# Between two layers of a fused diffusion block: the layer's output scaled as its bank is emptied, and the next layer's first weight halves split in other places and partly on GpSimd

## The reference, cut to what matters

```
h  = modulate(rmsnorm(x, norm_mix_pre), shift, scale)
z  = h @ w_in                                  # 24 tiles of 128 columns
m  = merge_branches(h, four mixers of z) @ w_o
x  = x + mod[2] * rmsnorm(m, norm_mix_post)
f  = conv_ffn(modulate(rmsnorm(x, norm_ffn_pre), ...)) # ends in @ w_down
x  = x + mod[5] * rmsnorm(f, norm_ffn_post)
```

## Time and profile before

| | |
|---|---|
| median of 3 runs | 1653.98 us (1651.18 to 1657.06) |
| the profiled execution's own time | 1649.58 us |
| its span, first to last instruction | 1647.8 us |
| TensorE busy | 1590.0 us, 96% |
| VectorE busy | 932.1 us, 57% |
| ScalarE busy | 789.6 us, 48% |
| GpSimd busy | 309.6 us, 19% |
| mean granted TensorE clock | 0.990 of full speed |
| chain that ended last | TensorE 70%, VectorE 3%, ScalarE 3% |

### The profile page before, as it was taken

How to read it: one execution, slowest core, us unless ns; L and a number is a source line. 1 busy time by engine, 2 the same in 40 slices (tenths; PEclk the granted TensorE clock), 3 DMA queues, 4 the chain that set the end, 5 groups by cost and what they waited for, 6 DMA issues and landing times.

```text
span 1647.8 us, 33059 instructions
## 1 busy us (share of the span) xinstructions
PE 1590.0 (96%) x14076; PEld 1323.8 (80%) x14076; DVE 932.1 (57%) x1481; ACT 789.6 (48%) x1299; POOL 309.6 (19%) x248
## 2 busy tenths in 40 slices
PE   8999999998899999999999999999989899999998
PEld 6788767777678887888888886987877789889987
DVE  5364455564465569655554225655776265677764
ACT  4322456473354266443443225525766344566653
POOL 0160234323110000212222000312352120012210
PEclk9999999999999999999999999999999899999999
DMA  9753334233852352322225343833413295555453
GB/s 332 201 164 102 101 105 160 75 103 96 268 201 89 107 193 76 103 96 84 98 69 111 105 125 125 262 128 116 147 52 130 55 317 169 187 172 180 164 189 133
DMA packets 213840, 234.41 MB, mean 142 GB/s; under 512 B 5888, under 2 KB 194688, under 8 KB 213696
## 3 DMA queue, kind: packets, MB, share of 16 engines
q1 hardware_dynamic: 194208, 191.14, 35.3%
q0 software_dynamic: 14880, 34.87, 7.9%
q10 hardware_dynamic: 4608, 6.29, 1.1%
HBM read 216.55 MB, written 15.73 MB: 141 GB/s over the span
## 4 chain that ended last, share of the span: by engine, by line
PE 70%; DVE 3%; issue 3%; ACT 3%; DMA 1%; POOL 0%; ACTq 0%; DVEq 0%; POOLq 0%
PE ps L2333 15%; PE ps L2335 15%; PE ps L2334 15%; PE ps L2795 2%; PE ps L2629 2%; PE ps L2641 2%; PE ps L2424 1%; PE ps L2681 1%; PE ps L2398 1%; PE ps L2399 1%; PE ps L2400 1%; PE ps L2603 1%; PE ps L2788 1%; PE ps L2790 1%; PE ps L2789 1%
## 5 line engine op out<-in xcount | busy, mean ns | idle before, releaser
L1062 ACT ACTIVATE whi<-ring 128x1024 fp32r<-128x1024 f32 (+1 forms) x262 | 274.4, 1052 | 488.7 <-PE ps L2335 428.2
L1607 DVE TENSOR_TENSOR wlo<-ring,whi 128x1024 fp32r<-128x1024 f32 (+1 forms) x262 | 327.4, 1254 | 176.2 <-ACT whi L1062 175.4
L2333 PE MATMUL ps<-H,whi 128*128 128x256 f32 (+1 forms) x640 | 214.7, 336 | 1.8 <-DVE wlo L1607 1.8
L2335 PE MATMUL ps<-H,wlo 128*128 128x256 f32 (+1 forms) x640 | 214.2, 335 | 0.0
L2334 PE MATMUL ps<-H,whi 128*128 128x256 f32 (+1 forms) x640 | 214.2, 335 | 0.0
L2333 PE MATMUL ps<-HR,whi 128*128 128x512 f32 (+1 forms) x568 | 202.1, 356 | 0.5 <-DVE wlo L1607 0.3
L2335 PE MATMUL ps<-HR,wlo 128*128 128x512 f32 (+1 forms) x568 | 198.3, 349 | 0.0
L2334 PE MATMUL ps<-HR,whi 128*128 128x512 f32 (+1 forms) x568 | 198.2, 349 | 0.0
L2333 PEld LDWEIGHTS ps<-H,whi 128*128 128x128 f32 x640 | 121.5, 190 | 14.0 <-issue 1.9
L2335 PEld LDWEIGHTS ps<-H,wlo 128*128 128x128 f32 x640 | 121.5, 190 | 12.3
L2334 PEld LDWEIGHTS ps<-H,whi 128*128 128x128 f32 x640 | 121.5, 190 | 12.2
(11 more groups left out here) (399 smaller groups left out, 3219.2 us busy)
## 6 DMA issues: line engine op xcount, KB each, us to landing
ring<-in_ffn_up SPq DMA_DIRECT2D x44, 1024.0 KB, 5.0
ring<-in_w_gate SPq DMA_DIRECT2D x32, 1024.0 KB, 5.7
ring<-in_ada_w SPq DMA_DIRECT2D x32, 1024.0 KB, 5.3
ring<-in_w_in SPq DMA_DIRECT2D x24, 1024.0 KB, 7.9
ring<-in_ffn_down SPq DMA_DIRECT2D x10, 1024.0 KB, 5.0
ring<-in_ffn_down SPq DMA_DIRECT2D x18, 512.0 KB, 3.6
ada<-in_ada_w SPq DMA_DIRECT2D x8, 1024.0 KB, 11.6
WB<-in_w_branch POOLq DMA_DIRECT2D x8, 1024.0 KB, 6.3
```

The source lines that it names most:

```text
L1062: act.activation(whi[HALF_SLOT[m]][:, 0:kn, :], ring_half(raw, half, kn), ACT.Copy).then_inc(hi_done, 1)
L1607: dve.tensor_tensor(wlo[HALF_SLOT[m]][:, 0:kn, :], ring_half(raw, half, kn), whi[HALF_SLOT[m]][:, 0:kn, :].bitcast(F32), ALU.subtract).the ...
L2333: pe.matmul(o[:, c0:c1], hi[:, i, :], part(0, k), start=(k == 0), stop=False)
L2335: last = pe.matmul(o[:, c0:c1], lo[:, i, :], part(0, k), start=False, stop=(k == kn - 1))
```

## The change

Five things, all between the last product of layer 0 and the first of layer 1:

1. ACT scales `F` by `amod[:, 3]` as it empties the bank, in two instructions of 256 columns per tile instead of one of 512. The residual's second step becomes one addition of 512 columns, `X = X + F`.
2. DVE's modulation biases and the gains of layer 1's first norm move from behind the residual into it, behind the addition of its fifth tile. The four small scales move ahead of layer 0's down projection.
3. ACT splits the first high part behind the square of the fifth tile, the second behind that of the sixth, and the third behind the root of the second norm.
4. The three low parts are made by GpSimd, behind its last product of layer 0 and ahead of layer 1's bias loads.
5. DVE counts the three halves as made and waits for them behind `norm_apply`.

```diff
+SPLIT_BEHIND = (4, 5)
...
@@ gpsimd, behind the loop over FT
+                if l == 0:
+                    first_z = half_no(("z", 1, Z_ORDER[0]))
+                    for m in range(first_z, first_z + SPLIT):
+                        raw, half = HALVES[m]
+                        pool.wait_ge(lo_done, m)
+                        pool.wait_ge(hi_done, m + 1)
+                        pool.tensor_tensor(wlo[HALF_SLOT[m]][:, :, :], ring_half(raw, half),
+                                           whi[HALF_SLOT[m]][:, :, :].bitcast(F32), ALU.subtract).then_inc(lo_done, 1)
@@ scalar
                 for i in range(KT if l else 0):
                     act.wait_ge(x_ready, 8 + i + 1)
                     square(YB[:, i, :], X[:, i, :])
+                    if i in SPLIT_BEHIND:
+                        split_until(half_no(("z", l, Z_ORDER[0])) + SPLIT_BEHIND.index(i) + 1)
                 if l:
+                    norm_root(l, 0)
                     split_until(half_no(("z", l, Z_ORDER[0])) + SPLIT)
-                    norm_root(l, 0)
...
                     square(SQF[:, j, c0:c1], s[:, c0:c1])
-                    act.activation(F[:, j, c0:c1], s[:, c0:c1], ACT.Copy).then_inc(frees(("down", l, j)), 1)
+                    if j == 0:
+                        act.wait_ge(gains_ready, 4 * l + 3)
+                    for x in streams(l):
+                        ins = act.activation(F[:, j, 256 * x:256 * x + 256], s[:, 256 * x:256 * x + 256], ACT.Copy,
+                                             scale=amod[:, 3, j, x:x + 1])
+                    ins.then_inc(frees(("down", l, j)), 1)
@@ vector, residual
-                        for s in streams(l):
-                            x = X[:, i - 1, 256 * s:256 * s + 256]
-                            ins = dve.scalar_tensor_tensor(x, O[:, i - 1, 256 * s:256 * s + 256],
-                                                           amod[:, k, i - 1, s:s + 1], x, ALU.mult, ALU.add)
+                        x = X[:, i - 1, c0:c1]
+                        if k == 3:
+                            ins = dve.tensor_tensor(x, x, O[:, i - 1, c0:c1], ALU.add)
+                        else:
...
                         ins.then_inc(x_ready, 1)
+                    if k == 3 and i == 5:
+                        fill(("end", l, 0))
+                        gains(l + 1, (0,))
@@ vector, start of a layer
-                if l:
-                    gains(l, (0,))
-                link(dve.tensor_scalar(omu[:, :], vc(l, "mu", 0, 14), -1.0, 1.0, ALU.mult, ALU.add))
...
-                if l:
-                    split_until(half_no(("z", l, Z_ORDER[0])) + SPLIT)
+                if l == 0:
+                    layer_scales(0)
+                else:
                     norm_apply(l, 0, X, Z, HR)
                     fill(("gap", l, 0))
+                    halves[0] += SPLIT
+                    dve.wait_ge(lo_done, halves[0])
@@ vector, ahead of the down projection
+                layer_scales(l + 1)
```

More of the change, by code:

```diff
@@ L1637, in _, with layer_scales @@
             called = [0]
+            def layer_scales(l):
+                link(dve.tensor_scalar(omu[:, :], vc(l, "mu", 0, 14), -1.0, 1.0, ALU.mult, ALU.add))
+                link(dve.tensor_scalar(oka[:, :], vc(l, "ka", 0, 2), -0.5, 1.0, ALU.mult, ALU.add))
+                link(dve.tensor_scalar(hka[:, :], vc(l, "ka", 0, 2), 0.5, None, ALU.mult))
+                link(dve.tensor_scalar(hwa[:, :], vc(l, "w0", 0, 8), 0.5, None, ALU.mult))
             def norm_apply(l, k, src, tmp, dst):
@@ L1669, in residual @@
                         dve.wait_ge(scaled, 8 * (2 * l + k // 2) + i)
-                        for s in streams(l):
-                            x = X[:, i - 1, 256 * s:256 * s + 256]
-                            ins = dve.scalar_tensor_tensor(x, O[:, i - 1, 256 * s:256 * s + 256],
-                                                           amod[:, k, i - 1, s:s + 1], x, ALU.mult, ALU.add)
+                        x = X[:, i - 1, c0:c1]
+                        if k == 3:
+                            ins = dve.tensor_tensor(x, x, O[:, i - 1, c0:c1], ALU.add)
+                        else:
+                            for st in streams(l):
+                                x = X[:, i - 1, 256 * st:256 * st + 256]
+                                ins = dve.scalar_tensor_tensor(x, O[:, i - 1, 256 * st:256 * st + 256],
+                                                               amod[:, k, i - 1, st:st + 1], x, ALU.mult, ALU.add)
                         ins.then_inc(x_ready, 1)
+                    if k == 3 and i == 5:
+                        fill(("end", l, 0))
+                        gains(l + 1, (0,))
             dve.memset(cpad[:, :, :], 0.0).then_inc(c_zero, 1)
@@ L1730, in _ @@
                 ns = len(streams(l))
-                if l:
-                    gains(l, (0,))
-                link(dve.tensor_scalar(omu[:, :], vc(l, "mu", 0, 14), -1.0, 1.0, ALU.mult, ALU.add))
-                link(dve.tensor_scalar(oka[:, :], vc(l, "ka", 0, 2), -0.5, 1.0, ALU.mult, ALU.add))
-                link(dve.tensor_scalar(hka[:, :], vc(l, "ka", 0, 2), 0.5, None, ALU.mult))
-                link(dve.tensor_scalar(hwa[:, :], vc(l, "w0", 0, 8), 0.5, None, ALU.mult))
-                if l:
-                    split_until(half_no(("z", l, Z_ORDER[0])) + SPLIT)
+                if l == 0:
+                    layer_scales(0)
+                else:
                     norm_apply(l, 0, X, Z, HR)
                     fill(("gap", l, 0))
+                    halves[0] += SPLIT
+                    dve.wait_ge(lo_done, halves[0])
                 for n, t in enumerate(Z_ORDER):
@@ L2280, in _ @@
                 residual(l, 3, F)
-                fill(("end", l, 0))
                 dve.wait_ge(x_ready, 16 * l + 16)
```

## The result

| | before | changed |
|---|---|---|
| median | 1653.98 us (5 runs, 1651.18 to 1657.06) | 1667.28 us (5 runs, 1665.05 to 1667.71) |
| ratio to before | | 1.0074, 95% interval 1.0057 to 1.0091 |
| the profiled execution | 1649.58 us, span 1647.8 | 1667.61 us, span 1665.8 |
| mean granted TensorE clock in it | 0.990 | 0.984 |

A ratio here is an estimate from the runs with its interval, not the quotient of the two medians (which is 1.0080). Ratios go by undisturbed executions: the only slow one in this document, 1679.56 us in e8, is left out of them.

What follows compares the result with a forecast made beforehand. TensorE, busy 1590.0 of 1647.8 us, bounds the kernel, so only its waits at the layer 0 to 1 seam count. Fillers +5.3, vanished row waits -1.1, sum +4.2: 1653.98 to 1658.2 us, range 1652 to 1663.5.

Steps and rivals of the forecast that it cites:

- The collision: In the residual, GpSimd's first two low parts each block VectorE through the shared port, costing the chain 2.2 us each.
- Rival B: Port does not bite at the residual: -0.2 us, 1653.8, or about +2 with one block; chance 0.21 with one block.
- The gate: Fillers wait behind root, third high part and slower GpSimd low part, starting at 25.1 instead of 19.8, +5.3 us.
- The sum without the clock: Whole seam between layers 0 and 1: +5.3 - 1.1 = +4.2 us, the granted clock not counted.
- The rows' waits: TensorE's waits for rows in layer 1's first three tiles vanish: 11.4 instead of 12.54 us, giving back 1.1.
- rival D: TensorE's clock falls before the fillers have ended: +4.2 and 2 to 5 us more, 1660 to 1663; chance 0.18.
- the walk: Step through the changed seam with one execution's durations: residual ends 18.0, root 19.9, fillers 25.1, first product 29.7.
- C: Gain at the seam: no blocking and GpSimd nearly as quick as VectorE (1.2), -1.4 us, 1652.6; chance 0.06.
- E: GpSimd's late, bunched loads starve a ring load in the first tiles: +1 to +3 us on top, 1660; chance 0.05.

Runs made afterwards that it cites:

- e8: As e4, but only the nine dummy products ahead of the seventh square, the second hole left bare; median 1660.97 us, ratio 1.0031.
- e10: The changed kernel, low parts still on GpSimd, with the third high part moved ahead of the second root; median 1661.04 us, ratio 1.0046.
- e3: The changed kernel with one more wait: GpSimd makes its three low parts only when the residual is finished; median 1656.43 us, ratio 1.0020.
- e4: The changed kernel with dummy TensorE products, nine ahead of the seventh square's wait and eight ahead of the fillers' wait; median 1655.75 us, ratio 1.0027.
- e12: As e1, with five dummy TensorE products in the second hole alone, ahead of the fillers' wait; median 1654.11 us, ratio 1.0004.
- e7: The kernel before again, no edit, for a second profile; median 1654.89 us, ratio 1.0004.
- e1: The changed kernel with the three low parts back on VectorE, between residual and first row; median 1655.28 us, ratio 1.0017.
- e6: The changed kernel again, no edit; median 1665.44 us over 12 runs, ratio 1.0059.
- e11: As e1, with the dummy products of e4 in both holes; median 1660.27 us, ratio 1.0034.
- e2: As e1, with the third high part also ahead of the second root; median 1651.02 us, ratio 0.9986.
- e5: The changed kernel's scaling, residual, gains and scales alone; halves split as in the kernel before, low parts on VectorE; median 1653.70 us, ratio 0.9996.

## Why the prediction was wrong

All in the prediction's own time (1000 left out, 1.39 taken off the changed kernel's places):

| step | forecast | measured |
|---|---|---|
| residual tile on VectorE | 1.21 | 1.21 |
| low part on GpSimd, 1024 wide | 2.4 | 2.54 to 2.6 (2.40 in e10, no VectorE operation beside it) |
| VectorE operation beside it | about 2.9, twice | 2.88, and 3.42 for a pair |
| residual ends | 18.0 | 18.05 |
| root | 19.9 | 21.99 |
| third low part | 22.6 to 25.0 | 24.43 to 26.97 |
| fillers start | 25.1 | 27.11 |
| first product of layer 1 | 29.7 | 34.33 |
| first product to fourth tile | 11.4 | 11.44 |
| fourth tile's first product | 41.2 | 45.77 |

**The collision** was forecast rightly, and it was the term that no row of the changed kernel's width showed. The straight line through the two narrower shapes gave 2.4 for 2.54 to 2.6, and 2.40 is what the low part took with VectorE idle (e10). The estimate of 2.1 from the Trainium skill's "GPSIMD Engine Reference", section Instruction dispatch, lies further below. The rule of the Trainium skill's "SBUF — State Buffer", section Who interferes with whom, now has its row at 1024 columns: 2.88 against 0.68, and e3 takes the block away by a wait. Rival B (the port does not bite) is refuted by both.

**The gate** (low part behind root, third high part and a slower engine) is right: the steps from root to fillers are 27.11 - 21.99 = 5.1 measured and 25.1 - 19.9 = 5.2 forecast. e10 shows it by moving it: the same root, and fillers 3.6 earlier. **The sum without the clock**, +4.2, was measured as +4.4 in e4. And e12 (37.24) against e4 (41.69), both at a clock of 1.00, puts all 4.45 of it on GpSimd. **The rows' waits** vanished as said (11.44 for 11.4).

**The step that failed is the clock.** The prediction saw it as rival D, "if the clock falls before the fillers have ended", at "2 to 5 more", and gave it a chance of 0.18. It should have been the forecast. In the sum the clock stood at nothing. The two jumps in the table are its work: 2.1 at the root, where the last sum took 3.78 instead of 1.98, and 2.6 more at the first product, where the fillers took 7.57 instead of 4.99. Of the 2.1, 0.3 is a size in the walk: at full clock, in e4, the root comes at 20.48 - 0.27 = 20.21 in the prediction's time, not at 19.9. Two errors lie in that step. The first: I looked only at the hole ahead of the fillers (2.4 to 3.8 us). The walk itself made a second hole: it let the residual stand still for 4.4 us, and TensorE, which lives on the squares there, with it. That hole of 4.41 was in my numbers (last square 14.49 to 18.1), and I priced it as lateness alone. The second: I argued "2.4 us cost nothing here" from one execution. e7 and e1 show falls behind 2.44 and 2.74 us, so a hole a good deal longer had to be taken as a fall. With D as the forecast, and both holes counted at what e4 shows them to have cost in the first profile, the sum would have been 4.2 + 4.35, some 1662.5.

**What remains.** The medians 1667.28 and 1665.44 are 13.3 and 11.9 above the kernel before in the same runs' time. The ratios put it at 12.2 (9.4 to 15.1) and 9.8 (6.6 to 12.9). The seam explains 8.8 and 7.8. The 8.8 lies under the first interval and the 7.8 inside the second, so whether the change costs 2 to 4 us outside the seam is open. Single executions cannot settle it: the part behind the seam took 618.6 in the changed kernel and 614.0 in e6, 610.8 and 614.8 in the two executions of the kernel before, and 620.1 in e4. In the runs' mean clocks the changed kernel has 0.984 and 0.985, the kernel before 0.990, so 8 to 10 us more of clock are missing over the span (0.005 and 0.006 of 1660), where the seam lacks 5 to 7 (46.0 x 0.15, 45.1 x 0.11). With the two holes filled (e4) the runs' mean clock is 0.989, and the whole time is 4.5 above the kernel before (1.2 to 7.8), as its seam's 4.4 says: there nothing is missing. e10 and e11 stand at 7.6 (3.3 to 11.9) and 5.6 (2.3 to 9.1), with seams of 3.9 and 3.3 over before, so the whole times are too wide to tell 2 to 4 us. That a later start shifts the phase in which layer 1's thin parts meet the clock is a guess that was not tried.

**Rivals.** C (a gain) was wrong from its premise on, a quick GpSimd. E (late loads): the bias loads did move from 885 and 899 to 1028.27 and 1037.72, and no engine on the chain waited for them. The bounds: D was outside the forecast's own case, and its upper end, 1663, carried only one fall. The range ended at 1663.5 for that reason, 3.8 under the median.

## What to carry to other kernels

Price a stretch in which another engine stalls twice: once as lateness, and once for every hole that it opens in TensorE, since the work behind the hole can run at half clock; a hole longer than one behind which the clock has been seen to fall in the same place is to be taken as a fall. Moving two-input work from VectorE to GpSimd freed nothing here while VectorE had two-input work of its own on the chain. And look at what stands ahead of a gate in each in-order queue: one high part moved ahead of the root gave 4 to 5 us of the seam with the low parts on either engine (e10, and e2 against e1). Some of that is clock; with the low parts on VectorE and the clock at 1.00 in both, it is 37.24 - 35.17 = 2.1 (e12 and e2).

## What the runs showed of the hardware that was not expected

- Two waiting engines took turns: GpSimd's second low part was ready behind its first, and still one VectorE operation went between (2.88 ended, then 3.42 for a pair). A low part on GpSimd kept to 2.5 to 2.6 beside VectorE (5.22 for two, 7.59 for three in e3); with VectorE idle it took 2.40 (e10). VectorE bore the loss: an operation of 0.68 took 2.88.
- The granted clock fell behind every empty hole of 3.3 to 4.5 us in the seam (changed kernel, e3, e6, e8, e10), behind 2.74 in e1, and behind 2.44 in one of two executions of the kernel before; it did not behind e5's 2.25. Whether the length of the hole decides, or the thin work ahead of it too, no run separates. Dummy products on TensorE in the holes kept it at 1.00 (e4, e12), at no cost where they were shorter than the hole (e12), and at 3.3 us of the seam where they were longer (40.53 in e11 against 37.24 in e12).
- Two executions of the kernel before differ by 16.8 us in their span, with mean clocks of 0.990 and 0.976 (e7). The ends of the residual repeat to 0.01 us meanwhile in executions of one kernel (14.72, 18.32, 13.97 and 13.98), so such landmarks, not the whole time, tell small changes apart.
